# Averaging the summed squares of two norms with f32r matmuls on a high and a low part, in a two-layer decoder kernel

## The reference, cut to what matters

```python
def rmsnorm(x, g):
    xf = x.astype(jnp.float32)
    y = xf * lax.rsqrt(jnp.mean(xf * xf, axis=-1, keepdims=True) + EPS)
    return (y * g.astype(jnp.float32)).astype(x.dtype)

    x = x + jnp.concatenate([y_ret, y_pool, y_ml], axis=-1) @ w_out
    h = rmsnorm(x, norm_ffn)
    gu = h @ w_gate_up
    x = x + (jax.nn.silu(gu[..., :D_FF]) * gu[..., D_FF:]) @ w_down
    hp = rmsnorm(x, norm_ple)
    x = x + jax.nn.sigmoid(hp @ w_ple_gate) * (p_i @ w_ple_proj)
```

## Time and profile before

| | |
|---|---|
| median of 3 runs | 2445.36 us (2444.49 to 2446.41) |
| the profiled execution, its own time | 2445.41 us |
| its span, first to last instruction | 2443.6 us |
| busy PE / DVE / ACT / POOL | 2414.4 / 1529.2 / 968.2 / 1225.4 us |
| TensorE clock granted, mean | 0.998 of full speed |

### The profile page before, as it was taken

The page is one execution under the profiler, slowest core; times in us unless marked ns, Lnnn a source line. Parts: engine busy times, 40 slices in busy tenths (PEclk is TensorE's granted clock), DMA queues, the critical chain, the costliest instruction groups (busy, mean ns, idle before and its releaser), DMA issues.

```text
span 2443.6 us, 30214 instructions
## 1 busy us (share of the span) xinstructions
PE 2414.4 (99%) x11528; PEld 1992.0 (82%) x11528; DVE 1529.2 (63%) x1946; ACT 968.2 (40%) x1424; POOL 1225.4 (50%) x772
## 2 busy tenths in 40 slices
PE   7999999999999999999999999999999999999998
PEld 6888878888888888888878887888888888788886
DVE  7967846555454467776596777546545444776745
ACT  5233335433333334446333352335333333343553
POOL 3211112178778868882221112212888788598710
PEclk9999999999999999999999999999999999999999
DMA  4342223123233255332143322312223233545211
GB/s 164 111 97 56 78 62 112 35 91 108 87 118 110 96 176 167 126 130 69 39 151 102 82 53 72 98 60 69 87 90 108 95 119 110 185 147 164 78 52 69
DMA packets 108415, 245.92 MB, mean 101 GB/s; under 512 B 35688, under 2 KB 44136, under 8 KB 104432
## 3 DMA queue, kind: packets, MB, share of 16 engines
q1 hardware_dynamic: 60880, 126.90, 17.0%
q10 hardware_dynamic: 47392, 117.09, 14.5%
HBM read 179.43 MB, written 51.41 MB: 94 GB/s over the span
## 4 chain that ended last, share of the span: by engine, by line
PE 96%; DVE 2%; ACT 1%; DMA 0%; issue 0%; POOL 0%; ACTq 0%; DVEq 0%; POOLq 0%
PE proj L2165 14%; PE proj L2167 14%; PE proj L2166 14%; PE proj L2228 5%; PE proj L2229 5%; PE proj L2227 5%; PE aux L2228 5%; PE aux L2229 5%; PE aux L2227 5%; PE proj L2261 3%; PE proj L2263 3%; PE proj L2262 3%; PE aux L2261 2%; PE aux L2263 2%; PE aux L2262 2%; PE aux L2378 1%
## 5 line engine op out<-in xcount | busy, mean ns | idle before, releaser
L2117 POOL TENSOR_TENSOR w_lo<-w_raw,w_hi 128x1024 fp32r<-128x1024 f32 x100 | 262.2, 2623 | 907.7 <-ACT w_hi L1561 907.6
L2165 PE MATMUL proj<-h_hi,w_hi 128*128 128x512 f32 x1376 | 546.2, 397 | 0.9 <-POOL w_lo L2117 0.9
L2167 PE MATMUL proj<-h_lo,w_hi 128*128 128x512 f32 x1376 | 536.1, 390 | 0.0
L2166 PE MATMUL proj<-h_hi,w_lo 128*128 128x512 f32 x1376 | 535.8, 389 | 0.0
L2124 POOL TENSOR_TENSOR w_lo<-w_raw,w_hi 128x512 fp32r<-128x512 f32 x180 | 274.8, 1530 | 120.4 <-ACT w_hi L1543 120.3
L2124 POOL TENSOR_TENSOR w_lo<-turns,w_hi 128x512 fp32r<-128x512 f32 x180 | 269.9, 1501 | 88.2 <-ACT w_hi L1543 88.2
L2165 PEld LDWEIGHTS proj<-h_hi,w_hi 128*128 128x128 f32 x1376 | 258.5, 188 | 57.6 <-issue 3.6
L2166 PEld LDWEIGHTS proj<-h_hi,w_lo 128*128 128x128 f32 x1376 | 258.6, 188 | 54.2 <-issue 2.9
L2167 PEld LDWEIGHTS proj<-h_lo,w_hi 128*128 128x128 f32 x1376 | 258.3, 188 | 54.4
L1543 ACT ACTIVATE w_hi<-turns 128x512 fp32r<-128x512 f32 x180 | 113.1, 628 | 228.0 <-PE proj L2229 99.1
L1543 ACT ACTIVATE w_hi<-w_raw 128x512 fp32r<-128x512 f32 x180 | 112.3, 627 | 223.4 <-PE aux L2229 93.2
(11 more groups left out here) (329 smaller groups left out, 5355.8 us busy)
## 6 DMA issues: line engine op xcount, KB each, us to landing
w_raw<-weights SPq DMA_DIRECT2D x160, 512.0 KB, 3.5
turns<-weights SPq DMA_DIRECT2D x60, 512.0 KB, 3.8
act_sums_spill<-rows ACTq DMA_DIRECT2D x20, 1024.0 KB, 6.8
h_whole<-act_sums_spill ACTq DMA_DIRECT2D x40, 512.0 KB, 4.0
act_sums_spill<-act ACTq DMA_DIRECT2D x20, 512.0 KB, 5.2
ffn_b_whole<-act_sums_spill ACTq DMA_DIRECT2D x20, 512.0 KB, 4.8
act_sums_spill<-act ACTq DMA_DIRECT2D x20, 256.0 KB, 4.3
ffn_bw_whole<-act_sums_spill ACTq DMA_DIRECT2D x10, 512.0 KB, 3.8
```

The costliest lines, as they stand in the source:

```text
L2117: g.tensor_tensor(wlo[:, slot, 0:n], w, whi[:, slot, 0:n].bitcast(F32), ALU.subtract).then_inc(weights_ready.sem, 1)
L2165: pe.matmul(out, wh, rhi, start=first, stop=False)
L2166: pe.matmul(out, wl, rhi, start=False, stop=False)
L2167: return pe.matmul(out, wh, rlo, start=False, stop=final)
```

## The change

The averages of the feed-forward norm and of the side-gate norm are made of f32r operands. Once, in layer 0, ACT copies `mean_all` into an f32r tile, `mean_r` ("mean_weights"); 1/1024 is a power of two. For each of the four norms (two in each layer) and each token half

- ACT copies the sum of squares into `acc_hi` (`sum_high`, which waits for the last two additions: 15 for half 0 and 16 for half 1);
- DVE subtracts it from the sum and leaves the rest in `acc_lo` (`split_sum`, which waits for ACT's copy);
- PE multiplies both by `mean_r` into the same bank, two matmuls where there was one, and waits for DVE's subtraction.

`acc_hi` lies over `squares`, `acc_lo` over `square_sum`. The mixing norm and the last norm stay as they were. In the side-gate norm half 0 was waited for at 14 additions, and now its copy waits for 15.

```diff
+        acc_hi = at("square_sum_hi", w_at + 16384, [P, 2, HALF], F32R)
+        acc_lo = at("square_sum_lo", w_at + 20480, [P, 2, HALF], F32R)
...
+            def split_sum(L, i, h):
+
+                v.wait_ge(acc_high.sem, acc_high.at(L, 2 * i + h - 1))
+                v.tensor_tensor(acc_lo[:, h, :], acc[:, h, :], acc_hi[:, h, :].bitcast(F32),
+                                ALU.subtract).then_inc(acc_split.sem, 1)
...
                 for j in range(8, 16):
                     ple_square(L, j)
+                split_sum(L, 2, 0)
+                split_sum(L, 2, 1)
...
                         ffn_low(L, 7, 1)
+                        split_sum(L, 1, 0)
+                        split_sum(L, 1, 1)
                         for c in range(0, KC, 2):
                             ffn_low(L, c, 1)
...
+            def sum_high(L, i, h, added):
+
+                a.wait_ge(sq_added.sem, added)
+                a.activation(acc_hi[:, h, :], acc[:, h, :], ACT.Copy).then_inc(acc_high.sem, 1)
...
+                        if L == 0:
+                            a.activation(mean_r, mean_all, ACT.Copy).then_inc(mean_made, 1)
                         a.wait_ge(h_ready.sem, h_ready.at(L, 32))
...
+                        sum_high(L, 1, 0, sq_added.at(L, 15))
+                        sum_high(L, 1, 1, sq_added.at(L, 16))
                         for c in range(0, KC, 2):
                             high_part(c, 1, gain(c), ffn_piece(c, 1)[0])
...
+                        sum_high(L, 2, 0, sq_added.at(L, 16 + 15))
+                        sum_high(L, 2, 1, sq_added.at(L, 16 + 16))
                         root(L, 2)
...
                 for h in sides:
-                    if L == 0 and base < 0:
+                    if i > 0:
+                        pe.wait_ge(mean_made, 1)
+                        pe.wait_ge(acc_split.sem, acc_split.at(L, 2 * i + h - 1))
+                    elif L == 0 and base < 0:
...
-                    pe.matmul(abank(name), mean_all, acc[:, h, :], start=True, stop=True).then_inc(aux_done.sem, 1)
+                    if i > 0:
+                        pe.matmul(abank(name), mean_r, acc_hi[:, h, :], start=True, stop=False)
+                        pe.matmul(abank(name), mean_r, acc_lo[:, h, :], start=False, stop=True).then_inc(aux_done.sem, 1)
+                    else:
+                        pe.matmul(abank(name), mean_all, acc[:, h, :], start=True, stop=True).then_inc(aux_done.sem, 1)
...
                             if k == 15:
-                                sums(L, 16, 2, early=14)
+                                sums(L, 16, 2)
```

More of the change, by code:

```diff
@@ L361, in build @@
         tmp16 = sb("tmp16", [P, 16])
+        mean_r = sb("mean_weights", [P, P], F32R)
         const_landed, pos_landed = sem("const_landed"), sem("pos_landed")
@@ L383, in build @@
         sq_added = Signal(sem("sq_added"), 48, 16)
+        acc_high = Signal(sem("square_sum_high"), 4)
+        acc_split = Signal(sem("square_sum_split"), 4)
+        mean_made = sem("mean_weights_made")
         made_b12 = Signal(sem("b12_made"), 4)
```

## The result

| | kernel before | changed kernel |
|---|---|---|
| median | 2445.45 us (21 executions, 2444.31 to 2448.57) | 2448.95 us (21 executions, 2446.91 to 2452.05) |
| ratio to the kernel before | 1 | 1.0013 (95% interval 1.0008 to 1.0019) |
| profiled execution, its own time | 2445.41 us | 2447.26 us |
| its span | 2443.6 us | 2445.5 us |

The change costs 3.5 us of median, 0.14%: small, but its interval lies clear of 1. It is inside the forecast's range (2444.7 to 2450.0), on the forecast side, and 2.15 us above the forecast value. The profiled execution, 2447.3 us, is close to that value. The two facts belong together, as the experiments show.

A forecast was written before the change was run, and what follows sets the result against it. PE was taken as the bound, busy 2414.4 of 2443.6 us. Saving 2 x 0.80 us in feed-forward norms and losing 2 x 1.5 us in side-gate norms gave +1.4 us on 2445.41: 2446.8 us, range 2444.7 to 2450.0.

The forecast's parts named there:

- The feed-forward norm: Averages behind a fill of 24 matmuls: f32r form without a wait, 0.80 us saved in each of two norms.
- 0.8 us of slack at the wait: Feed-forward norm: DVE's subtractions end at 475.70, PE asks for them at 476.52, so no wait.
- ACT's and DVE's 1.2 us of delay: Feed-forward norm: ACT and DVE up to `rstd` run 1.2 to 1.3 us late, covered; without cover 1.25 us a layer.
- The late second matmul: Behind the averages: next unit's second matmul starts 0.63 us after 477.83, counted to the fp32 form within its 1.71 us.
- The side-gate norm's stop: Averages right after the sixteenth fill: PE stands still 2.1 us, the norm costs 1.5 us more in each layer.
- `rstd` later by 1 us at no cost: Behind the side-gate norm: `rstd` comes 1.0 us later, but its first reader waits for PE's fill; costs nothing.
- The sum, 2446.8 us: Whole kernel: -2 x 0.80 in feed-forward norms, +2 x 1.5 in side-gate norms, +1.4 us on 2445.41 us.
- rival 1: Side-gate norm: the stop costs the clock, 2448.4 us if once, 2450.0 us in both layers; chance 12%.
- a stop of 1.9 us behind dense work: Trace before, 2102.20 to 2104.13: clock stayed at 1.00 behind it, cited against the clock falling after the 2.1 us stop.
- the prediction's own signs: New profile: right if granted clock after the side-gate stop reads 1.00, wrong if 0.5 or the stop is far from 2.1 us.
- The rival of the faster side: Side-gate norm: no stop if high parts run ahead of the sixteenth copy, all 3.2 us saved, 2442.2 us; chance 3%.
- Within 0.2%: Whole kernel: change within 0.2%, or 4.9 us, given 95%; less than that can't be told from no change.

The follow-up runs named there:

- ffn_only: Changed kernel's f32r form in the feed-forward norm alone, the side-gate norm left in fp32: 2443.8 us against 2445.8 for the kernel before, ratio 0.9992.
- highs_earlier: Changed kernel with the side-gate norm's two high parts ahead of ACT's fourteenth copy: 2443.65 us against 2445.47 for the kernel before, ratio 0.9993.
- sums_behind_fill: Changed kernel with the side-gate norm's averages behind the gate's first fill: 2441.9 us against 2445.8 for the kernel before, ratio 0.9984.
- fp32_waits: Changed kernel with the side-gate norm multiplying in fp32, still waiting for high part and subtraction: 2450.45 us against 2445.47 for the kernel before, ratio 1.0021.
- stop_filled: Changed kernel with eight more f32r matmuls on PE in the side-gate norm's stop, results overwritten: 2447.05 us against 2445.58 for the kernel before, ratio 1.0005.
- gate_only: Changed kernel's f32r form in the side-gate norm alone: 2450.6 us against 2445.8 for the kernel before, ratio 1.0019.
- after_again: The changed kernel unaltered, measured once more on the same chip as `stop_filled`: 2449.98 us against 2445.58 for the kernel before, ratio 1.0012.
- after: The changed kernel itself: median 2448.95 us against 2445.45 for the kernel before, ratio 1.0013; its profiled execution 2447.26 us.
- highs_first: Changed kernel with the side-gate norm's two high parts ahead of ACT's sixteenth copy: 2445.9 us against 2445.8 for the kernel before, ratio 1.0001.
- stop_longer: Changed kernel with two more unread ACT copies ahead of the side-gate norm's high parts: 2452.7 us against 2445.47 for the kernel before, ratio 1.0029.

## Why the prediction was right or wrong

- **The feed-forward norm**: right. Averages of 0.91 us were forecast and are 0.92 us; 0.8 us of slack at the wait was enough; ACT's and DVE's 1.2 us of delay reached nothing on PE (`ffn_only`). The late second matmul, which the forecast counts to the fp32 form, is no cost of its own but a part of the fourth record's 0.43 us; the 1.71 us are right.
- **The side-gate norm's stop**: right. The first average was to start 2.09 us after PE asked and starts 2.14 us after it; the second half at 2.69 us and 2.74 us; the norm was to cost 1.5 us more and costs 1.55 us. That it is the place in ACT's queue, and neither the form nor the work, is shown by `highs_earlier` and `sums_behind_fill` on one side and `fp32_waits` on the other.
- **`rstd` later by 1 us at no cost**: right, and with room: in `sums_behind_fill` it comes later still, at no cost to PE.
- **The sum, 2446.8 us**: the value of an execution at the full clock (`stop_filled` 2447.05 us, the profiled one 2447.26 us), not of the median. The step that failed is the chance of rival 1, 12% for the half clock behind the stop. I argued from a stop of 1.9 us behind dense work that left the clock alone, took the stop's length for the whole matter and one execution for all. The same trace even had a harmless stop longer than the forecast one, 2.17 us in the start-up (30.44 us, granted clock 1.00 behind it), so the length gave no warning either. Stops of 1.98 us lose the clock in one execution (`gate_only`, with 0.58 and 0.62 granted behind them; `after_again`, with 0.73 and 0.64) and keep it in another (`after`, `fp32_waits`: 1.00 behind both), so here such a stop can cost the clock and need not. By the prediction's own signs it holds in the profiled execution and fails in those where the clock reads half behind the stop. Its price was right, 1.6 us a time. The 1.6 us are read from the start-up of the trace before: from 16.49 to 19.64, at 0.50 granted, 7 intervals take 3.15 us in place of 1.59; behind a stop `gate_only` shows 3.38 us for 8 intervals in place of 1.81. A drop in one layer at the median would be 1.5 + 1.6 = 3.1 us; measured are 3.5 and 4.4 us in two sessions, with drops in neither layer of one trace and in both of the other.
- **The rival of the faster side**: its time was right and its condition was not. High parts ahead of the sixteenth copy were to give 2442.2 us; `highs_first` does just that and takes 2445.9 us, and ahead of the fourteenth copy it is 2443.65 us. What reached 2441.9 us was another change of order, the averages behind a fill.
- **Within 0.2%**: right, at 0.14%. That no less than 0.2% could be told from no change was too careful: with 21 executions of each kernel the interval of 1.0008 to 1.0019 lies clear of 1.

Left open: how often each single stop loses the clock. The executions give only a mean clock, and only one of them in each run has a trace.

## What to carry to other kernels

A step that shortens a matmul by adding work on other engines is worth its saving only where that work can end before PE asks: ask what stands ahead of it in its engine's queue, and whether that itself waits for PE's last matmul. If so, no slack of the data helps, and either the work goes further up the queue or PE gets something else to do first (here one fill, worth 7 us between two orders of the same instructions, the clock's share included). A stop of PE of about 2 us can be paid twice, once by the wait and once by the clock (here, with 1.98 us of idle PE, the norm took 1.55 us more, and 1.6 us more again where the clock fell), and one profiled execution can miss the second half.

## What the runs showed of the hardware

- The second payment is not the same in every execution: with the same 1.98 us of idle PE the matmuls behind it ran 0.227 us apart in one trace of the changed kernel and 0.43 us apart in another, in both layers. With 3.0 us of idleness they did so in both layers of the one trace taken, and the median rose by a further 2.7 us (against `after_again`) or 3.7 us (against the changed kernel's first median), where the added wait is 2.1 us.
- The length of a stop doesn't decide it alone. Every kernel here also has a stop in the start-up, ahead of the mixing norm's average at 30.4 us. Of five traces with 3.3 us there, two have the half clock behind it (`stop_longer`, `highs_first`: 0.64 and 0.67 in the stretch 30 to 34 us) and three don't (`ffn_only`, `after_again`, `sums_behind_fill`: 1.00); of seven with 0.8 to 2.4 us one has it (`gate_only`, 1.98 us, 0.59).
- Useless matmuls in the stop made the program faster by 2.9 us (2447.05 against 2449.98 us in one session; 2.3 us in the means of 11 executions each), with the wait as long as before.
- An fp32 matmul of 128x512 shows as two records 0.43 us apart, 0.86 us in all, against 0.227 us for an f32r one. The f32r matmul behind it is recorded early, while the last fp32 record still runs, so that its successor looks late (0.63 us); what the averages cost is the four records' 1.71 us, or 1.80 us behind a stop (`fp32_waits`).
